# The expert gather of a two-block model on one core: 28 diagonal buffers in place of 8, and VectorE's dependent steps behind drain instructions in place of counted increments

## What is computed

```python
def block(xb):                                   # 256 tokens; 8 heads, K = 16
    q = (xb @ w_q).reshape(TOK_BLOCK, PEER_HEADS, 2, PEER_DHALF)
    s = jnp.einsum('thcd,hcnd->thcn', q, sub_keys).astype(jnp.float32)
    top_s, top_i = lax.top_k(s, K)
    cand = top_s[:, :, 0, :, None] + top_s[:, :, 1, None, :]
    best_s, best_c = lax.top_k(cand.reshape(TOK_BLOCK, PEER_HEADS, K * K), K)
    i1 = jnp.take_along_axis(top_i[:, :, 0], best_c // K, axis=-1)
    i2 = jnp.take_along_axis(top_i[:, :, 1], best_c % K, axis=-1)
    e = (i1 * PEER_NKEYS + i2).reshape(TOK_BLOCK, PEER_HEADS * K)
    gate = jax.nn.softmax(best_s, axis=-1).reshape(TOK_BLOCK, PEER_HEADS * K)
    u = expert_u[e]
    act = jax.nn.gelu(jnp.einsum('td,ted->te', xb, u), approximate=False)
    coef = (gate * act.astype(jnp.float32)).astype(xb.dtype)
    return jnp.einsum('te,ted->td', coef, expert_v[e])
```

## Time and profile before

| | us |
|---|---|
| median of 3 runs (lowest to highest) | 1626.83 (1622.99 to 1627.62) |
| the profiled execution, its own time | 1618.75 |
| its span, first to last instruction | 1617.0 |
| first gather issued | 873.11 |
| last gather issued | 1600.60 |

### The profile page before, as it was taken

The page is one execution under the profiler, slowest core; times in us unless marked ns, Lnnn a source line. Parts: engine busy times, 40 slices in busy tenths (PEclk is TensorE's granted clock), DMA queues, the critical chain, the costliest instruction groups (busy, mean ns, idle before and its releaser), DMA issues.

```text
span 1617.0 us, 22190 instructions
## 1 busy us (share of the span) xinstructions
PE 1375.2 (85%) x8206; PEld 991.4 (61%) x8206; DVE 1040.8 (64%) x2068; ACT 564.7 (35%) x1048; POOL 531.6 (33%) x620
## 2 busy tenths in 40 slices
PE   8999999997999999999999757766777838786776
PEld 7988998896999888788888623322322313232222
DVE  5657765488776557977776957576655547474444
ACT  6656654466665444232441220212121211112011
POOL 8200010000000000000002667666666666666664
PEclk9999999998999999999999979978988969898898
DMA  8445665544565553312265999999999999999997
GB/s 252 146 143 161 186 206 189 182 131 139 174 196 197 192 163 104 99 56 80 93 234 181 381 383 381 380 368 352 362 376 366 383 359 380 399 356 349 387 370 280
DMA packets 184014, 408.93 MB, mean 253 GB/s; under 512 B 10674, under 2 KB 91868, under 8 KB 183916
## 3 DMA queue, kind: packets, MB, share of 16 engines
q0 software_dynamic: 74096, 269.52, 43.5%
q1 hardware_dynamic: 109516, 137.06, 26.3%
q10 hardware_dynamic: 304, 1.05, 0.2%
HBM read 406.54 MB, written 1.05 MB: 252 GB/s over the span
## 4 chain that ended last, share of the span: by engine, by line
PE 48%; POOL 22%; issue 14%; DVE 10%; another core or an unknown queue 3%; DMA 2%; ACT 1%; DVEq 0%; ACTq 0%; POOLq 0%
PE banks L2254 11%; PE banks L2255 11%; PE banks L2256 11%; POOL arena L914 10%; POOL wring L914 7%; POOL h_raw L914 3%; PE banks L2770 3%; PE banks L2498 3%; PE banks L2733 2%; POOL sq L914 2%; PE banks L2595 1%; PE banks L2489 1%; DVE w_a_low L1412 1%; DVE arena L2089 1%
## 5 line engine op out<-in xcount | busy, mean ns | idle before, releaser
L2770 PE MATMUL banks<-arena 128*128 128x512 f32 x416 | 230.8, 702 | 136.5 <-issue 110.5
L914 POOL DMA_INDIRECT arena<-in_expert_u_dram,eidx x117 | 110.7, 946 | 690.4 <-DVEq L2073 636.1
L1412 DVE TENSOR_TENSOR w_a_low<-wring,w_a_high 128x1024 fp32r<-128x1024 f32 x192 | 235.5, 1230 | 121.8 <-ACT w_a_high L957 117.0
L1376 ACT ACTIVATE arena<-ident,arena 128x128 f32<-128x128 f32 x238 | 87.1, 396 | 513.2 <-remote 386.2
L2770 PEld LDWEIGHTS banks<-arena 128*128 128x128 f32 x416 | 87.4, 222 | 277.3 <-issue 250.0
L957 ACT ACTIVATE w_a_high<-wring 128x1024 fp32r<-128x1024 f32 x192 | 201.1, 1052 | 123.9 <-PE banks L2256 121.4
L2254 PE MATMUL banks<-h_high,w_a_high 128*128 128x256 f32 (+1 forms) x832 | 238.4, 287 | 0.9 <-DVE h_low L1434 0.6
L2255 PE MATMUL banks<-h_low,w_a_high 128*128 128x256 f32 (+1 forms) x832 | 235.3, 283 | 0.0
L2256 PE MATMUL banks<-h_high,w_a_low 128*128 128x256 f32 (+1 forms) x832 | 233.8, 281 | 0.0
L2089 DVE CUSTOM_DVE_ANT_0 arena<-arena,banks 128x1024 f32<-128x1024 f32 x117 | 140.6, 1216 | 48.5 <-DMA arena<-in_expert_u_dram,eidx 37.0
L2770 PE MATMUL banks<-wring,arena 128*128 128x512 f32 x308 | 142.4, 609 | 21.5 <-issue 19.1
(11 more groups left out here) (404 smaller groups left out, 2351.1 us busy)
## 6 DMA issues: line engine op xcount, KB each, us to landing
wring<-in_mlp_w_dram SPq DMA_DIRECT2D x64, 1024.0 KB, 5.4
wring<-in_w_in_dram SPq DMA_DIRECT2D x19, 1024.0 KB, 5.7
wring<-in_sb_w_qkv_dram SPq DMA_DIRECT2D x11, 1024.0 KB, 7.5
wring<-in_rg_w_in_dram SPq DMA_DIRECT2D x8, 1024.0 KB, 5.5
wring<-in_w_q_dram SPq DMA_DIRECT2D x8, 1024.0 KB, 5.4
wring<-in_sb_w_o_dram SPq DMA_DIRECT2D x4, 1024.0 KB, 5.2
wring<-in_rg_w_o_dram SPq DMA_DIRECT2D x4, 1024.0 KB, 5.3
wring<-in_w_o_dram SPq DMA_DIRECT2D x4, 1024.0 KB, 7.4
```

Of the source, the lines that this page charges most:

```text
L914: g.indirect_dma_start(out=grow(j), out_offset=None, in_=(expert_u, expert_v)[which][0], in_offset=bass.IndirectOffsetOnAxis(ap=eidx[:, tt ...
L1376: a.activation(diag[:, n % DIAGS, :], ident[:], ACT.Copy, scale=coef[:, tt, c0 + r:c0 + r + 1]).then_inc(diag_ready, 1)
L1412: v.tensor_tensor(unit(n, 1), raw_unit(n), unit(n, 0).bitcast(F32), ALU.subtract).then_inc(w_split, 1)
L2770: last = mm(y_banks[tt][half][:, :], diag[:, n % DIAGS, :], grow(j)[:, 512 * half:512 * (half + 1)], start=False, stop=True, skip_group_ch ...
```

## The change

`DIAGS` is 28: diagonals 0 to 7 keep their memory, 8 to 27 lie where two of the old scratch rows and the end of the queries' memory were. All of DVE's scratch is now one row, `junk`. Every step of `choose`, `shares` and `coefficients`, and every `dot_row`, begins with `dve.drain()`; the increments of `dve_chain` in them are gone, and so are the waits of `dot_row` for its own earlier rows and for the scores' banks.

```diff
-DIAGS = 8
+DIAGS = 28
...
-        junk_first = [area(20552, D), yacc[0]]
-        junk = [area(20552, D), area(4096, D), area(5120, D), area(27942, D)]
+        junk = area(20552, D)
...
-        diag = area(2048, DIAGS, P)
+        diag = [area(2048 + P * j if j < 8 else 4096 + P * (j - 8), P) for j in range(DIAGS)]
...
-                settle()
+
+                dve.drain()
                 if step == 0:
                     wait_out(dve, f"sc{tt}_{h0}")
                     for k in range(2 * nh):
-                        last = v.max(vals[:, k, 0:8], scored[:, k, :])
-                    mark(last)
+                        v.max(vals[:, k, 0:8], scored[:, k, :])
...
-                tt, c, n = b // 4, BSEL * (b % 4) + r, BSEL * b + r
+                tt, c = b // 4, BSEL * (b % 4) + r
                 j, before = gather_row(b, 0, r)
-                scratch = junk if b else junk_first
-                back = len(scratch)
-                if n == BSEL:
-                    wait_out(dve, *[f"sc1_{2 * m}" for m in range(4)])
-                if r >= back:
-                    jb, before_b = gather_row(b, 0, r - back)
-                    dve.wait_ge(slot_free[jb], before_b + 1)
+                dve.drain()
                 dve.wait_ge(row_loaded[j], 16 * (before + 1))
-                v.tensor_tensor_reduce(out=scratch[r % back], in0=grow(j), in1=f_bank[tt][:, :], scale=1.0, scalar=0.0,
+                v.tensor_tensor_reduce(out=junk, in0=grow(j), in1=f_bank[tt][:, :], scale=1.0, scalar=0.0,
                                        op0=ALU.mult, op1=ALU.add,
                                        accum_out=dots[:, tt, c:c + 1]).then_inc(slot_free[j], 1)
...
-                settle()
+                dve.drain()
                 dve.wait_ge(gelu_ready, b + 1)
```

More of the change, by code:

```diff
@@ L1375, in _ @@
                             act.wait_ge(slot_free[j], before + 1)
-                        a.activation(diag[:, n % DIAGS, :], ident[:], ACT.Copy,
+                        a.activation(diag[n % DIAGS], ident[:], ACT.Copy,
                                      scale=coef[:, tt, c0 + r:c0 + r + 1]).then_inc(diag_ready, 1)
@@ L2001, in times @@
                         oo = o_[:, TOPK * i:TOPK * (i + 1), :]
-                        last = v.tensor_tensor(oo, oo, topf[:, 2 * (h0 + i) + half, :].unsqueeze(1).broadcast_to(
+                        v.tensor_tensor(oo, oo, topf[:, 2 * (h0 + i) + half, :].unsqueeze(1).broadcast_to(
                             [P, TOPK, TOPK]), ALU.mult)
-                    mark(last)
-                settle()
+                dve.drain()
                 if step == 0:
@@ L2014, in choose @@
                         v.max_index(idx[:, k, 0:8], vals[:, k, 0:8], scored[:, k, :])
-                        last = v.match_replace(rest[:, k, :], vals[:, k, 0:8], scored[:, k, :], NEG)
-                    mark(last)
+                        v.match_replace(rest[:, k, :], vals[:, k, 0:8], scored[:, k, :], NEG)
                 elif step == 2:
                     for k in range(2 * nh):
-                        last = v.max(vals[:, k, 8:16], rest[:, k, :])
-                    mark(last)
+                        v.max(vals[:, k, 8:16], rest[:, k, :])
                 elif step == 3:
@@ L2024, in choose @@
                     for i in range(nh):
-                        last = v.tensor_tensor(sums[:, i, :].rearrange("p (i j) -> p i j", j=TOPK),
+                        v.tensor_tensor(sums[:, i, :].rearrange("p (i j) -> p i j", j=TOPK),
                                                vals[:, 2 * i, :].unsqueeze(2).broadcast_to([P, TOPK, TOPK]),
@@ L2032, in choose @@
                     for i in range(nh):
-                        last = v.max(best[:, i, 0:8], sums[:, i, :])
-                    mark(last)
+                        v.max(best[:, i, 0:8], sums[:, i, :])
                 elif step == 5:
@@ L2037, in choose @@
                         v.max_index(at[:, i, 0:8], best[:, i, 0:8], sums[:, i, :])
-                        last = v.match_replace(rest2[:, i, :], best[:, i, 0:8], sums[:, i, :], NEG)
-                    mark(last)
+                        v.match_replace(rest2[:, i, :], best[:, i, 0:8], sums[:, i, :], NEG)
                 elif step == 6:
                     for i in range(nh):
-                        last = v.max(best[:, i, 8:16], rest2[:, i, :])
-                    mark(last)
+                        v.max(best[:, i, 8:16], rest2[:, i, :])
                 elif step == 7:
@@ L2769, in _ @@
                     for half in range(2):
-                        last = mm(y_banks[tt][half][:, :], diag[:, n % DIAGS, :],
+                        last = mm(y_banks[tt][half][:, :], diag[n % DIAGS],
                                   grow(j)[:, 512 * half:512 * (half + 1)], start=False, stop=True,
```

27 lines of the change are left out of this document (13 added, 14 removed).

## The result

The changed kernel takes 1631.0 us (median of 7; 1625.2 to 1633.7), the kernel before 1624.6 (7 runs beside it; 1622.9 to 1627.6). The ratio is 1.0032 with a 95% interval of 1.002 to 1.0044: slower by 5 to 6 us. Forecast were 1616 us and a gain.

A forecast was written before the change was run, and what follows sets the result against it. The prediction took POOL's gather issue and its stalls as the bound. Terms of -10, -2 and +1 us gave -11 us, from a median of 1626.8 to 1616 us, range 1582 to 1636.

The forecast's parts named there:

- The bound: In the gather, POOL sets the pace; its stalls are increments seen late while the DMA engines run at their ceiling.
- whatever takes stalls from POOL shortens the kernel: In the gather: only removing POOL's stalls, 90 us beyond its usual gaps, makes the kernel faster.
- The ring, -10 us: ACT's diagonals: 28 buffers nearly end its 386.2 us of remote waits, PE turns prompt, POOL stalls less; ends 0 and 80.
- nothing: Rival, chance 0.24: PE's increments, not its promptness, stop POOL in the gather; all stays within 5 us of 1627.
- Increments and waits that go, -2 us: DVE's dots and steps: 186 increments and 226 waits fewer; earlier expert numbers spare POOL some stalls; ends 0 and -9.
- Drains that come, +1 us: DVE's steps and dots: 459 drains at 0.12 us each, 55 us mostly covered by 294 us spare.
- Slower: Rival, chance 0.18: drains at every dot make DVE late in busy stretches, u slots stop POOL; +34 us, 1661.
- Large: Rival, chance 0.18: fewer DVE increments let PE's arrive in time; half to nearly all of POOL's 90 us go, 1547 to 1585.
- The signs given: Profile after: POOL idle 233 us, wrong above 250 or under 215, or if drains cost DVE over 0.5 us each.

The follow-up runs named there:

- the ring alone: Kernel before with DIAGS raised from 8 to 28 and its scratch rows moved, nothing else; ratio 0.9991 to the kernel before.
- drains from block 1 on: Changed kernel with the old increments and waits in all DVE work until the end of block 0, drains after it; ratio 1.0009 to the kernel before.
- one matmul per row: Kernel before with PE doing only the first of a v row's two matmuls, same increments; ratio 1.0004 to the kernel before.
- the drains alone: Changed kernel with DIAGS back at 8; ratio 1.0028 to the kernel before.
- two drains: Changed kernel with two drains at every dot; ratio 1.0038 to the kernel before.
- drains until the end of block 0 alone: Kernel before with 28 diagonals and drains only in what DVE does until block 0 ends; ratio 1.0023 to the kernel before.
- dots in place: Kernel before with 28 diagonals, dots writing their product over the u row in its slot; steps keep increments and waits; ratio 0.9983 to the kernel before.
- POOL unheld: Kernel before with POOL waiting only for the slot's last landing, PE and DVE reading a constant row; ratio 1.1239 to the kernel before.

## Why the prediction was wrong

**The bound** was read rightly: the kernel goes at POOL's pace, and its stalls make the difference. Its cause was not: I put the late increments down to the DMA engines' ceiling. At a share of 0.65 they are as late. What the runs show is that from the end of block 0 on, in long stretches in which POOL issues back to back, DVE's and ACT's instructions come at one per 1.4 us once a few are behind, and PE's increments at one per 11.2 us. What the cause is stays open; at 900 to 910 us, with POOL issuing as fast, none of it is seen. Hence "whatever takes stalls from POOL shortens the kernel" is half true. Take the reason of one stall away and the next reader's work that is not done yet makes another: blocks 1 to 6 take 87 to 97 us each in every kernel in which readers hold POOL, with drains or without, with half of PE's matmuls or all, with half the bytes or all.

**The ring, -10 us.** The mechanism on ACT was right (diagonals in runs of 23 to 25, "remote" waits 4.5 us), the term mis-sized: 0.9991 is -1.5 us, and nothing is inside the interval. The low end of the range, zero, was the better value, for the reason that the rival "nothing" gave: PE's promptness does not decide.

**Increments and waits that go, -2 us.** For the dots' waits the runs give 0.9983 against 0.9991, -1.3 us, not to be told from nothing. For those of the steps there is no gain: drains in their place made the start longer.

**Drains that come, +1 us: the step that failed.** The drains cost 4.5 us against before by themselves (1.0028) and, with the ring, 6.7 against the ring alone. Two sentences failed. First, "On the path lie the 18 steps ahead of the first gather" and "a few at the end": the steps there (they are 38) cost 0.59 us, less than I gave them, but the steps and dots of block 0 from row 9 on lie on the path too, as far as the dot of row 11 and the one behind it, and block 1 begins 2.4 us later for it. I had set all work of DVE within the gather against its 294 us to spare, an average over stages. The earlier trace rows showed 2.1 us of idle time ended by dots, and I took it for nothing; the row of 910.03 stood in the same timeline. Second, "what is late there is the increment and not DVE's own work". A step without any increment was followed by a drain of 9.2 us. DVE's own instructions are what is late, a drain waits for all of them, and with one ahead of every dot 0.60 us each in the mean came out, five times the 0.12. In blocks 1 to 6 of the changed kernel DVE never caught up: no dot ended less than 23.0 us behind the end of its gather instruction, where before each of these blocks had one at 4.7 to 13.8.

Behind block 0 the drains are worth the rest, 2 to 3 us (1.0009 with drains from block 1 on, 0.9991 without: 2.9 us between them, which the intervals allow to be nothing). That it is DVE's lateness that costs them is argued and not shown: with one matmul per row the dots are 23.1 us behind on average and the time is that of before, and in the drains alone and with two drains DVE caught up in blocks 4 to 6 (dots at 9.8 to 14.7 us) and lost as much. Where in blocks 1 to 7 it is made the runs don't tell: one trace each is no finer than 2 to 3 us there. Why drains until the end of block 0 alone cost 5.2 us above the ring alone, when their trace shows 2.6 of it, is open too; the two intervals allow any difference from 1.1 us on, and the two kernels ran on different chips.

The Trainium skill (VectorE: DVE Perf Modes, "The DRAIN you can't avoid") says that a semaphore after each operation costs nothing extra. By that, dropping increments and waits is worth nothing, and the -1.3 us without the dots' waits can be told neither from that nor from my -2. On a drain instruction in their place the runs decide: ahead of the first gather, with POOL silent, 38 steps take 9.88 us with increments and 10.47 with drains.

**The rivals.** "Slower" named the right mechanism, dots a few microseconds late that stop POOL where PE's rows did before: 47.9 us of its idle time. Its price of +34 us was wrong because it added the dots' stalls to PE's; they took their place, 78.3 + 2.1 us became 51.5 + 47.9. "Nothing" came nearest by its number, since 1631.0 lies within 5 us of 1627, though the rise of 0.32% is clear of noise; its reason, that PE's promptness does not decide, held for the ring. "Large" is out: with the ring, and no dot waiting for another at all (dots in place), 2.7 us were gained. The stall at 1418.04 was no good witness against it, as it lies in block 6, where DVE still chooses for block 7.

**The signs given.** POOL's idle time was to be 233 us, and wrong above 250, "then look for dots": 260.7, and dots. Drains over 0.5 us: 0.60. DVE without "remote" waits at the steps: yes. PE with no stands of 7 us: no, it waits for diagonals up to 14.3 us at a block's start, because gelu and coefficients stand behind the late dots.

## What to carry to other kernels

Before you set work against an engine's spare time, look for the one place where another engine waits for it: some three microseconds, about half of this change's loss, were made in the first block, and 294 us of spare time did not cover them. When one stage paces the rest and its stalls are the only time in which the others come on, removing a reader's wait moves the stall to the next reader; try it with no reader holding it at all, and see whether what remains is shorter. And a drain is as long as the work ahead of it: put it where little is open. Drains in front of every dot cost little here as long as the steps had none (0.9999), and drains in both cost 6.7 us above the ring alone, so measure the halves together.

## What the runs showed that was not expected

- From block 1 on, in long stretches in which POOL issues gathers back to back (1.24 us each), DVE and ACT instructions that wait for nothing follow each other at 1.40 us. PE's increments come every 11.2 us for rows of 8 records and every 5.6 for rows of 4. Half the bytes (share 0.65) or half the rows per gather leave DVE's 1.40 as it is, and make the 11.2 us 10.5. At 900 to 910 us, in block 0, none of this is seen, though POOL issues as fast.
- With POOL unheld the gather is longer (871 us against 728, of which 42 are in the first block with its wait for the constant row), although POOL issues without stalls.
- A POOL memset of 0.12 us between two gathers lies in their 0.30 us gap and leaves them 1.24 us apart.
- Two drains in a row cost what one does (the second has a median of 19 ns).
- Open: every time here is of an execution whose instructions were recorded, so that the runs can't tell whether the 1.40 us would be there without records. The Trainium skill (NOTIFIC — the notification-queue block, "The write path") says that a full record queue can be set to stall the engine that writes to it, and that the runtime has it drop records instead; no run here shows either. The number of records alone does not explain it: at 900 to 910 us, where nothing was late, the windows count 154 instructions in 10 us, and at 1040 to 1050, where things were, 52.
